# One block of a transformer pair on one core: the value projections of the difference attention move inside its loop over heads

## What is computed

```python
def diff_mixer(h, cos, sin, w_in, lam_p, subln_g, w_out, layer):
    q, k, v = jnp.split(h @ w_in, [DIFF_QK_W, 2 * DIFF_QK_W], axis=-1)
    ...
    lam = exp(sum(lp[0] * lp[1])) - exp(sum(lp[2] * lp[3])) + lam_init
    o = diff_attention(q[..., 0, :], q[..., 1, :], k[..., 0, :], k[..., 1, :], v, lam)
    o = rms_norm_2(o, subln_g) * (1.0 - lam_init)
    return o.reshape(B, T, DIFF_V_W) @ w_out

def attention_of_one_block(qb1, qb2, k1, k2, v, lam, mask, scale):
    a1 = masked_softmax(einsum('bqhd,bkhd->bhqk', qb1, k1) * scale, mask)
    a2 = masked_softmax(einsum('bqhd,bkhd->bhqk', qb2, k2) * scale, mask)
    return einsum('bhqk,bkhd->bqhd', a1 - lam * a2, v)
```

## Time and profile before

| | us |
|---|---|
| median of 3 runs | 2444.02 (2442.82 to 2446.55) |
| profiled execution, its own time | 2441.23 |
| its span | 2439.4 |
| PE busy | 2262.5 (93%) |
| DVE / ACT / POOL busy | 1230.0 / 1117.0 / 695.5 |
| mean granted clock of PE | 0.942 of 2.4 GHz |

### The profile page before, as it was taken

The page is one execution under the profiler, slowest core; times in us unless marked ns, Lnnn a source line. Parts: engine busy times, 40 slices in busy tenths (PEclk is TensorE's granted clock), DMA queues, the critical chain, the costliest instruction groups (busy, mean ns, idle before and its releaser), DMA issues.

```text
span 2439.4 us, 30052 instructions
## 1 busy us (share of the span) xinstructions
PE 2262.5 (93%) x10896; PEld 1833.6 (75%) x10896; DVE 1230.0 (50%) x2214; ACT 1117.0 (46%) x1958; POOL 695.5 (29%) x460
## 2 busy tenths in 40 slices
PE   7988899989999999988989999999986888999997
PEld 5755688868888887766767888887865776788886
DVE  6776544447999634555444322324538455323223
ACT  5465633456888635545243232323737334332221
POOL 5150223310000222411323332323822324333232
PEclk9889999888999999988979999998999988999998
DMA  4310133216999530210211322231320221322221
GB/s 159 113 53 1 40 104 104 78 70 236 391 392 390 204 104 27 78 61 27 87 44 61 104 94 97 90 101 52 104 69 1 70 70 35 103 91 99 95 95 52
DMA packets 71650, 258.87 MB, mean 106 GB/s; under 512 B 7952, under 2 KB 8080, under 8 KB 71120
## 3 DMA queue, kind: packets, MB, share of 16 engines
q1 hardware_dynamic: 66816, 238.76, 27.8%
q0 software_dynamic: 2816, 11.82, 1.3%
q10 hardware_dynamic: 1872, 6.37, 0.7%
HBM read 245.36 MB, written 11.56 MB: 105 GB/s over the span
## 4 chain that ended last, share of the span: by engine, by line
PE 80%; DVE 7%; ACT 6%; issue 3%; POOL 2%; DMA 1%; POOLq 0%; DVEq 0%; SPq 0%; ACTq 0%
PE ps L506 16%; PE ps L507 16%; PE ps L508 16%; PE ps L565 3%; PE ps L1111 3%; PE ps L2679 2%; PE ps L2681 2%; PE ps L2680 2%; PE ps L1126 2%; PE ps L542 2%; PE ps L543 2%; PE ps L548 2%; PE ps L1145 2%; PE ps L2706 1%; PE ps L2707 1%
## 5 line engine op out<-in xcount | busy, mean ns | idle before, releaser
L448 ACT ACTIVATE wh<-raw 128x1024 fp32r<-128x1024 f32 x308 | 322.3, 1055 | 489.2 <-PE ps L508 463.8
L453 DVE TENSOR_TENSOR wl<-raw,wh 128x1024 fp32r<-128x1024 f32 x180 | 241.5, 1348 | 541.5 <-ACT wh L448 535.3
L506 PE MATMUL ps<-hh,wh 128*128 128x512 f32 (+1 forms) x1192 | 470.9, 395 | 8.2 <-POOL wl L453 7.9
L507 PE MATMUL ps<-hl,wh 128*128 128x512 f32 (+1 forms) x1192 | 467.7, 392 | 0.0
L508 PE MATMUL ps<-hh,wl 128*128 128x512 f32 (+1 forms) x1192 | 467.5, 392 | 0.0
L453 POOL TENSOR_TENSOR wl<-raw,wh 128x1024 fp32r<-128x1024 f32 x128 | 308.6, 2411 | 507.7 <-ACT wh L448 496.0
L506 PE MATMUL ps<-act,wh 128*128 128x512 f32 (+1 forms) x688 | 273.7, 398 | 11.0 <-ACT act L1386 9.9
L507 PE MATMUL ps<-act,wh 128*128 128x512 f32 (+1 forms) x688 | 272.0, 395 | 0.0
L508 PE MATMUL ps<-act,wl 128*128 128x512 f32 (+1 forms) x688 | 271.5, 395 | 0.0
L506 PEld LDWEIGHTS ps<-hh,wh 128*128 128x128 f32 (+1 forms) x1192 | 225.9, 190 | 57.9 <-issue 10.3
L508 PEld LDWEIGHTS ps<-hh,wl 128*128 128x128 f32 (+1 forms) x1192 | 225.6, 189 | 48.5 <-issue 0.2
(11 more groups left out here) (463 smaller groups left out, 3933.7 us busy)
## 6 DMA issues: line engine op xcount, KB each, us to landing
raw<-d_w SPq DMA_DIRECT2D x277, 512.0 KB, 3.3
raw_x<-d_moe SPq DMA_DIRECT2D x84, 512.0 KB, 6.6
raw<-d_moe SPq DMA_DIRECT2D x84, 512.0 KB, 6.8
d_xs<-Sb POOLq DMA_DIRECT2D x7, 514.0 KB, 8.2
Xb<-d_xs ACTq DMA_DIRECT2D x6, 514.0 KB, 6.8
area<-d_mem POOLq DMA_DIRECT2D x3, 1024.0 KB, 5.4
d_ys<-rows ACTq DMA_DIRECT2D x6, 512.0 KB, 6.1
xT<-d_x SPq DMA_DIRECT2D x8, 256.0 KB, 6.6
```

The costliest lines, as they stand in the source:

```text
L448: me.e.activation(hi, raw, ACT.Copy).then_inc(*me.done("wh", m))
L453: me.e.tensor_tensor(lo, raw, hi.bitcast(F32), ALU.subtract).then_inc(*me.done("wl", m))
L506: me.e.matmul(bank[0:m, 0:n], wh[:, c], hi, start=k == 0, stop=False)
L507: me.e.matmul(bank[0:m, 0:n], wh[:, c], lo, start=False, stop=False)
```

## The change

The loop over the eight value projections is gone from all four programs, and each projection, its copy, its transposes and its multiplication now stand in the loop over heads: projection n + 1 at the end of PE's step n, transposes of the values n in the middle of that step, ACT's copy and the split of a weight tile between the first and the second exponentials, DVE's multiplication at the end of its step. The projections and the values' transposes take their banks from `turns` (two banks) instead of `ps`. The input is thus still read inside the loop, so the second probabilities of odd heads no longer lie over it but in the angle tables `tab`; the second maxima and exponentials of heads 0 and 1 wait for the last rotation (`tok`, `dqk`, 15).

```diff
--- before.py
+++ after.py
@@ -488,8 +488,8 @@
     return (K.wh[:, 0, :], K.wl[:, 0, :]) if K.plan.dry else K.halves(tile)
 
 
-def linear(K, me, key, name, layer, columns, src, m=128, n=T, row0=0, after=None):
-    bank = K.banks[me.take("ps", *key)]
+def linear(K, me, key, name, layer, columns, src, m=128, n=T, row0=0, after=None, pool="ps"):
+    bank = K.banks[me.take(pool, *key)]
     for k, (hi, lo, ready) in enumerate(src):
         b = block(K, me, lo is not None, (name, layer, row0 + 128 * k, columns))
         tile, c = b // 8, slice(b % 8 * 128, b % 8 * 128 + m)
@@ -516,7 +516,7 @@
                 mm.then_inc(*me.done("mm", *key))
                 me.alias(*key)
     if after is not None:
-        me.give("ps", key, *after)
+        me.give(pool, key, *after)
     return bank
 
 
@@ -930,14 +930,14 @@
 
 
 
-def values_turn_pe(K, me, st, items, n, ntile):
+def values_turn_pe(K, me, st, items, n, ntile, pool="ps"):
     m = items[n]["m"]
-    bank = K.banks[me.take("ps", "turn", st, n)]
+    bank = K.banks[me.take(pool, "turn", st, n)]
     me.wait_ge("vc", st, n)
     for i in range(ntile):
         tp = me.e.transpose(bank[:, m * i:m * i + m], K.tan("vc", st, n)[0:m, 128 * i:128 * i + 128], K.ident[0:m, 0:m])
     tp.then_inc(*me.done("turn", st, n))
-    me.give("ps", ("turn", st, n), ("val", st, n))
+    me.give(pool, ("turn", st, n), ("val", st, n))
 
 
 def values_pe(K, me, st, items, ntile=NQ, ticks=0):
@@ -3483,7 +3483,7 @@
                       for r in (slice(0, 64), slice(64, 128))]
         K.i_diff.append(it)
     K.first = [K.S[:, 0, :, :], K.O[:, :, :]]
-    K.other = [K.S[:, 1, :, :], K.S_h[:, 0:NQ, :]]
+    K.other = [K.S[:, 1, :, :], K.tab[:, :, :]]
     K.lam, K.gs = K.mis[:, 2:3], K.mis[:, 3:4]
 
 
@@ -3587,7 +3587,7 @@
 
 
 def second_free(n):
-    return [("comb2", n - 2)] if n >= 2 else [("end", "pe", (("ffn", 0), 2))]
+    return [("comb2", n - 2)] if n >= 2 else [("end", "pe", (("ffn", 0), 2)), ("tok", "dqk", 15)]
 
 
 def diff_values_pe(K, me, m):
@@ -3603,6 +3603,11 @@
     mm.then_inc(*me.done("pv", "diff", m))
 
 
+def diff_value_pe(K, me, n):
+    it = K.i_vd[n]
+    linear(K, me, ("L", "vd", n), it["weight"], 0, it["cols"], it["src"], after=[("vc", "vd", n)], pool="turns")
+
+
 def diff_features_pe(K, me, m):
     bank = K.banks[me.take("turns", "feat", m)]
     me.wait_ge("scaled", m)
@@ -3615,18 +3620,22 @@
 def diff_pe(K, me):
     h = K.h("n6")
     heads_pe(K, me, "dqk", "od_w_in_2", h, K.i_dqk, "n6", 3)
-    values_pe(K, me, "vd", K.i_vd)
     me.set_apart("ps", "turns", 2)
-    for n in range(2):
-        diff_products_pe(K, me, n, K.i_diff[n])
-    for n in range(1, 10):
+    diff_products_pe(K, me, 0, K.i_diff[0])
+    diff_value_pe(K, me, 0)
+    for n in range(10):
         if n + 1 < 8:
             diff_products_pe(K, me, n + 1, K.i_diff[n + 1])
-        if n < 9:
+        if 1 <= n < 9:
             diff_turn_pe(K, me, n - 1, K.i_diff[n - 1], K.first[(n - 1) % 2], ("comb2", n - 1))
+        if n < 8:
+            values_turn_pe(K, me, "vd", K.i_vd, n, NQ, pool="turns")
+        if 1 <= n < 9:
             diff_values_pe(K, me, n - 1)
         if n >= 2:
             diff_features_pe(K, me, n - 2)
+        if n + 1 < 8:
+            diff_value_pe(K, me, n + 1)
     me.put_back("ps", "turns")
     me.alias("hfree", "n7")
     me.alias("end", "pe", "diff")
@@ -3646,7 +3655,7 @@
 
 def diff_act(K, me):
     heads_act(K, me, "dqk", K.i_dqk, "n6", 3)
-    values_act(K, me, "vd", K.i_vd)
+    ahead(K, me, ("L", "vd", 0))
     me.wait_ge("lambda", "lsum")
     me.e.activation(K.mis[:, 4:6], K.mis[:, 0:2], ACT.Exp).then_inc(*me.done("lambda", "lexp"))
     for n in range(11):
@@ -3654,6 +3663,9 @@
             diff_squares_act(K, me, n - 2)
         if n < 8:
             diff_exp_act(K, me, n, K.i_diff[n], K.first[n % 2], first_free(n), 0)
+            values_copy_act(K, me, "vd", K.i_vd, n, NQ)
+            if n + 1 < 8:
+                ahead(K, me, ("L", "vd", n + 1))
             diff_exp_act(K, me, n, K.i_diff[n], K.other[n % 2], second_free(n), 1)
         if 1 <= n < 9:
             diff_turned_copy(K, me, n - 1, K.i_diff[n - 1], pt_free("diff", n - 1, first_free(0)))
@@ -3710,7 +3722,7 @@
 
 def diff_dve(K, me):
     heads_dve(K, me, "dqk", K.i_dqk, "n6", 3)
-    values_dve(K, me, "vd", K.i_vd, norm="n6")
+    ahead(K, me, ("L", "vd", 0))
     diff_lambda_dve(K, me)
     for n in range(11):
         if n < 8:
@@ -3722,8 +3734,12 @@
             diff_gained_dve(K, me, n - 3)
         if 2 <= n < 10:
             diff_scaled_dve(K, me, n - 2)
+        if n + 1 < 8:
+            ahead(K, me, ("L", "vd", n + 1))
         if 1 <= n < 9:
             diff_turned_copy(K, me, n - 1, K.i_diff[n - 1], pt_free("diff", n - 1, first_free(0)))
+        if n < 8:
+            values_out_dve(K, me, "vd", K.i_vd, n, NQ, "n6")
     me.alias("end", "dve", "diff")
     war = [("end", w, "diff") for w in ("pe", "act")]
     sandwich_dve(K, me, "x7", 56, ("x", ("ffn", 0)), "n7", war, "mem2")
@@ -3748,13 +3764,15 @@
 
 def diff_pool(K, me):
     heads_pool(K, me, "dqk", K.i_dqk)
-    values_pool(K, me, "vd", K.i_vd)
-    for n in range(2, 11):
-        if n < 10:
+    ahead(K, me, ("L", "vd", 0))
+    for n in range(11):
+        if 2 <= n < 10:
             diff_root_pool(K, me, n - 2)
         if n >= 3:
             m = n - 3
             lo_of(K, me, ("dt", m), K.act[:, m, :], K.act[:, 8 + m, :], K.tdn("gained", m))
+        if n + 1 < 8:
+            ahead(K, me, ("L", "vd", n + 1))
     mem_load(K, me, "mem2")
     sandwich_pool(K, me, "x7", ("x", ("ffn", 0)), "n7", "mem2")
```

## The result

The changed kernel takes **2416.14 us** (median of 4 runs, 2414.47 to 2416.62); the kernel before, run beside it, 2443.42 (4 runs, 2439.11 to 2446.55). The ratio is 0.9907, with a 95% interval of 0.9884 to 0.993: faster by 17 to 28 us. The forecast was 2424.4 in 2418 to 2432. Run once more in the first group of experiments, the same kernel had a median of 2419.12 (6 runs, 2406.62 to 2432.72) beside 2442.03: ratio 0.9904 (0.9874 to 0.9935).

A forecast was written before the change was run, and what follows sets the result against it. PE alone bounds the value projections; elsewhere PE and ACT wait for each other in turns. First step 13.3, five of 13.74 and the end save 19.6 us off the median 2444.02: 2424.4, range 2418 to 2432.

The forecast's parts named there:

- The step: Loop over heads: one closed chain through PE and ACT sets the period, 13.7 us a head against 14.8.
- What lies beside it: DVE's and POOL's work in a loop step: about 11 of 13.7 us on DVE, with slack where PE waits.
- POOL's low half: Weight split on POOL, 2.38 us in each second step: can hold back the root by 2.4 us.
- The start: First heads: PE stands 3.0 us, first products at half clock last 4.64, projection 1 ends at 1787.6.
- POOL's wait of 2.29 us: PE's wait at 1778.74 for POOL's low half: goes, since its tile is now wanted at 1795.
- The sum: Whole stage: first step 13.3, five of 13.74, then the end, finishing at 1888.9 against 1908.5: 19.6 us saved.
- the end: After projection 7: 6.8 us to 1876.4, squares and root to 1879.8, then 9.07 to the output projection.
- Half clock in part: Rival, loop steps: PE's idle 1.4 us brings slow matmuls, 1.6 us a step, 9.8 in six; result 2434; chance 0.08.
- half clock throughout: Rival, whole loop at half clock: 6.6 us more a step, 46 in seven, result near 2470; chance 0.03.
- Serial: Rival, loop: projections find no cover, step stays 14.8; only the start is won, 13 us, result 2431; chance 0.07.
- Nothing: Rival, whole stage: an unseen wait (two banks, shared tables) eats the rest; result 2444; chance 0.04.

The follow-up runs named there:

- start_only: Changed kernel with only the last two value projections inside the steps of heads 0 and 1, six ahead of the attention: stretch 128.1 us, ratio to before 0.9982.
- copy_late: Changed kernel with ACT's copy of the value projection and the weight split behind both exponentials: stretch 115.8 us against 119.1, ratio to before 0.9872.
- late_from_1: Changed kernel with ACT's projection copy and weight split behind both exponentials for heads 1 to 7 only: stretch 115.2 us, median 2410.81 us, ratio to before 0.9891.
- again: The changed kernel run once more, unchanged: stretch 119.0 us, median 2419.12 us, ratio to before 0.9904.
- split_late2: Changed kernel with ACT's weight split behind the turned copies and DVE's half behind its values' multiplication: stretch 116.0 us, ratio to before 0.9899.
- lambda_late: Changed kernel with the computation of lambda moved behind head 0's maxima: stretch 119.4 us, ratio to before 0.9929.
- split_late: Changed kernel with only ACT's half of the weight split moved behind the turned copies: stretch 133.1 us, ratio to before 0.9957.

## Why the prediction was right

*The step.* Forecast 13.74, measured 13.48 to 13.50 in four steps, 12.98 in the first, and 12.55 in the last, which has no split. The sum had ten terms; the two copies of ACT were too long by a little and the three last transposes of the turned block too short. ACT's 0.60 for a copy is not the time that it holds the next operation: L960 starts at 1783.83 and L448 at 1784.32, 0.49 later, and 0.42 in the chain above. From the projection's last matmul to L448 the chain has 0.57 (1810.21 to 1810.78), against 0.25 + 0.60, and from the turned copy to the transposes 0.53, against 0.65: 0.4 less. The transposes, 0.38 and 0.47, measured 0.55 and 0.44, 0.14 more; the 0.55 stood in the earlier trace rows already.

*What lies beside it.* In the loop no wait of L3512 for DVE's combination showed, and no wait of L506 for the values (behind the loop, head 7's transposes wait 1.43 us for the combination, at 1872.64). This held, but with less to spare than forecast: in the step at 1814 the maxima are done 3.6 us into the projection, not 2.2, and the combination 1.7 before PE wants it, not 3.0. The longer L3558 (last section) takes most of that. POOL's low half did not hold back the root visibly to PE.

*The start.* Right within half a microsecond in each part that was named: the first scores at half clock, 4.64; the wait in front of them 3.16 (forecast 3.0); the second scores 11.3 us after L907's end (forecast 10.9); projection 1 done after 19.6 (forecast 19.2). POOL's wait of 2.29 us is gone. That the scores took just 4.64 is luck in part: behind the same wait four other traces have 3.84 to 4.03 (last section).

*The sum.* From L907's end to the first matmul of the output projection: 19.6 + 13.0 + 67.5 + 18.6 = 118.7, against 19.2 + 13.3 + 68.7 + 19.3 = 120.5. The 1.8 between, by which the stage became 21.4 shorter and not 19.6, are the steps (1.5) and the end (0.7), less the start (0.4). The mechanism was right; the most mis-sized term is the step. That the median fell 1.9 below the range is this and the scatter of a program in which the same last L907 starts anywhere between 1763.3 and 1778.3 in these traces: the range was made from the terms of the stage and from three runs of before that differed by 3.7 us, while 23 runs of it later spread over 22 (2431.6 to 2453.97). The range should have been wider by that.

*The rivals.* Half clock in part and half clock throughout: the granted clock is 1.00 over 79.5 us with a wait of 1.07 in each step, so neither took place in the loop. The Trainium skill (TensorE: Matmul & The Clock Gate, A second HAM failure mode: psum-queue depth-cycling) made this loop of two banks the one to fear; the trace disagrees, twice, with the loop of before and with this one. Serial: the steps gained 9.5, and start_only alone, 12.4, is well short of the whole. Nothing: the ratio's interval excludes it.

*Not foreseen.* That the two halves of the change give 5.6 us more apart than together, which the experiments alone show: I had priced the bare 3.16 us and the half clock behind it as a fact, not as something that the change itself puts there. And that the order of ACT could shorten the stretch by 3 to 4 us more (copy_late, late_from_1): the second exponentials fed the chain, and the copy that stood in front of them did not have to. Whether that shows in the whole time is open: the ratios don't separate it.

## What to carry to other kernels

In engines that work in order, a step's period is the longest closed chain through all of them; write it down link by link, and put independent matmuls where PE would wait, but put the copies that they need behind whatever feeds the chain. A producer and its consumer on another engine have to be moved together: the same move of ACT's split cost 14 us with DVE's half left in place, and gained 3 with it moved along. Filling work is a fixed amount: what covers a wait at the start is missing at the end, and of the 5.9 us moved to the start here 1.8 was left.

## What the runs showed of the hardware

Tiny operations of DVE were stretched beside POOL. The changed kernel's timeline, POOL, DVE and one line of ACT:

```profile
1767.79 1.72 POOL L756 TENSOR_TENSOR area<-td,tab 128x512 f32<-128x512 f32 x1
1768.30 1.28 DVE L3683 CUSTOM_DVE_ANT_0 mis<-small 128x64 f32<-128x64 f32 x1
...
1769.63 0.22 DVE L3685 CUSTOM_DVE_ANT_0 mis<-small 128x64 f32<-128x64 f32 x1
...
1817.19 0.69 DVE L3553 CUSTOM_DVE_ANT_0 Sb<-ps,const 128x512 f32<-128x512 f32 x1
1817.44 2.40 POOL L453 TENSOR_TENSOR wl<-raw,wh 128x1024 fp32r<-128x1024 f32 x1
...
1817.92 1.94 DVE L3558 TENSOR_SCALAR stat<-stat 128x4 f32<-128x4 f32 x1
...
1819.90 0.40 ACT L3570 ACTIVATE Sb<-Sb,stat 128x128 f32<-128x128 f32 x1 [0.91 <-DVE stat L3558]
```

L3558 works on 128x4 numbers, takes 0.17 us by itself, and here 1.94: it ends at 1819.86, just as POOL's L453 does (1819.84). At 1773.15 it took 0.24 and ended with POOL's L453 again (1773.39 and 1773.37). L3683 and L3685 are the same operation; the one that starts within POOL's L756 takes 1.28, the other 0.22, and in the kernel before, where POOL is idle at that point, both take 0.22. L3553, which reads PSUM, keeps its 0.69 while L453 begins. Over all 16 executions of L3558 in each kernel (shortest, median, longest in ns), first of the changed one:

```profile
L3558 DVE TENSOR_SCALAR stat<-stat x16: 170/170/1943, 1773.2 to 1860.2; 128x4 f32<-128x4 f32 x16
```

and of the kernel before:

```profile
L3558 DVE TENSOR_SCALAR stat<-stat x16: 170/170/482, 1822.4 to 1887.5; 128x4 f32<-128x4 f32 x16
```

The Trainium skill (SBUF — State Buffer, Who interferes with whom) says that DVE and POOL share a pair of ports, that a DVE operation which uses it (a `tensor_scalar` can; one with two inputs in SBUF does against a POOL operation that reads SBUF) and one of POOL lock each other out of it, and that whoever starts first has it for the whole instruction. The rows agree, with 1.94 instead of 0.17 us; I had not expected it of operations this small. No run here removed POOL's split to test it. It makes ACT wait 0.91 us for the first exponentials in such a step, which the projection covers: these two steps last 13.49 us like the others, so it costs the time nothing here.

The other thing is that like waits leave unlike clocks. The first scores stand behind the same wait in seven traces, 3.15 or 3.16 us, and took 4.64 in the changed kernel, again and split_late2, but 4.03 in lambda_late, 4.00 in split_late, 3.99 in copy_late and 3.84 in late_from_1. At the end, the product that takes 2.40 in the changed kernel took 3.66 in lambda_late, 4.25 in start_only. With one trace of each kernel, this can't be put down to the edits. Whole times show the same: of 23 runs of the kernel before on one chip, the fastest (2431.6 us) had a mean granted clock of 0.948 and the slowest (2453.97) one of 0.936. Whether the clock makes the time or waits make both, no run here decides.
